# Two transformer blocks of two layers on one core: signs, a constant scale and row factors moved within the softmax steps

## What is computed

```python
# first block, top-k attention ("b") and differential attention ("c"); q and k are RMS-normalised
logits = einsum('bqhd,bqshd->bhqs', qb, k_sel) * DSA_HD ** -0.5
p = softmax(where(valid, logits, -inf))                       # "b"
logits = einsum('bqhcd,bshcd->bhcqs', qb, k) * DIFF_HD ** -0.5
p = softmax(where(allowed, logits, -inf))
attn = p[:, :, 0] - lam * p[:, :, 1]                          # "c"
# second block: scale = 1 / sqrt(64) = 1/8
q = rope(rms_norm(q, q_norm), pos)
s_c = einsum('bsghd,bngd->bsghn', q, k_cmp) * scale           # compressed keys
o_s = softmax(where(m, einsum(q, kg) * scale, NEG)) @ vg      # selected blocks
o_w = softmax(where(mw, einsum(q, kw) * scale, NEG)) @ vw     # window
o = g[..., 0:1] * o_cmp + g[..., 1:2] * o_s + g[..., 2:3] * o_w
```

## Time and profile before

| | |
|---|---|
| median of three runs | 2692.9 us (2691.5 to 2694.1) |
| the profiled execution: its own time | 2695.4 us |
| its span in the trace | 2693.6 us |
| TensorE matmuls busy | 2487.0 us, 92% |
| VectorE busy | 1395.3 us, 52%, 2981 instructions |
| ScalarE busy | 954.4 us, 35% |
| GpSimd busy | 879.1 us, 33%, 366 instructions |
| mean granted TensorE clock | 0.964 |

### The profile page before, as it was taken

How to read it: one execution, slowest core, us unless ns; L and a number is a source line. 1 busy time by engine, 2 the same in 40 slices (tenths; PEclk the granted TensorE clock), 3 DMA queues, 4 the chain that set the end, 5 groups by cost and what they waited for, 6 DMA issues and landing times.

```text
span 2693.6 us, 34184 instructions
## 1 busy us (share of the span) xinstructions
PE 2487.0 (92%) x12299; PEld 1989.3 (74%) x12303; DVE 1395.3 (52%) x2981; ACT 954.4 (35%) x1691; POOL 879.1 (33%) x366
## 2 busy tenths in 40 slices
PE   7998999899999899989988888999998888899999
PEld 6686877678868687767877557888887655788887
DVE  4587243554468734355377445454567754523335
ACT  4342243432444224343234543322224354332221
POOL 3242414234324241423422102444543200244442
PEclk9999999999999999999999889999998998999999
DMA  5232414125423241413532102444433100233332
GB/s 174 66 94 71 164 32 141 48 91 181 134 70 94 94 149 40 126 47 110 176 82 66 31 1 63 149 151 154 160 118 101 57 17 1 71 105 99 96 100 79
DMA packets 132173, 256.00 MB, mean 95 GB/s; under 512 B 21914, under 2 KB 28588, under 8 KB 132012
## 3 DMA queue, kind: packets, MB, share of 16 engines
q1 hardware_dynamic: 132012, 253.83, 29.8%
HBM read 249.60 MB, written 4.19 MB: 94 GB/s over the span
## 4 chain that ended last, share of the span: by engine, by line
PE 76%; DVE 16%; ACT 4%; issue 3%; DMA 0%; DVEq 0%; SPq 0%; ACTq 0%
PE ps L758 63%; PE ps L712 4%; PE ps L1009 1%; PE ps L905 1%; DVE arena L1705 1%; PE ps L1055 1%; DVE nsm L1418 1%; DVE top L1703 1%; PE ps L820 1%; PE ps L885 1%; DVE nsm L1416 1%; DVE ps L1644 1%; PE ps L880 1%; DVE ps L1642 1%; ACT arena L1367 1%
## 5 line engine op out<-in xcount | busy, mean ns | idle before, releaser
L688 POOL TENSOR_TENSOR wl<-raw,wh 128x1024 fp32r<-128x1024 f32 (+2 forms) x362 | 878.9, 2433 | 1788.1 <-ACT wh L1076 1787.2
L758 PE MATMUL ps<-wh,hTh 128*128 128x512 f32 (+3 forms) x1600 | 639.7, 400 | 1.2 <-DVE hTl L1648 1.2
L758 PE MATMUL ps<-wh,hTl 128*128 128x512 f32 (+3 forms) x1600 | 620.3, 388 | 0.0
L758 PE MATMUL ps<-wl,hTh 128*128 128x512 f32 (+3 forms) x1600 | 620.3, 388 | 0.0
L1076 ACT ACTIVATE wh<-raw 128x1024 fp32r<-128x1024 f32 (+2 forms) x362 | 378.4, 1049 | 522.4 <-PE ps L758 278.0
L758 PEld LDWEIGHTS ps<-wh,hTh 128*128 128x128 f32 x1600 | 307.3, 192 | 75.6 <-issue 19.7
L758 PEld LDWEIGHTS ps<-wh,hTl 128*128 128x128 f32 x1600 | 306.7, 192 | 59.5
L758 PEld LDWEIGHTS ps<-wl,hTh 128*128 128x128 f32 x1600 | 307.5, 192 | 51.3
L758 PE MATMUL ps<-hTh,wh 128*128 128x512 f32 (+2 forms) x704 | 259.0, 368 | 5.2 <-DVE hTl L1648 2.4
L758 PE MATMUL ps<-hTh,wl 128*128 128x512 f32 (+2 forms) x704 | 257.8, 366 | 0.0
L758 PE MATMUL ps<-hTl,wh 128*128 128x512 f32 (+2 forms) x704 | 257.7, 366 | 0.0
(11 more groups left out here) (271 smaller groups left out, 3251.0 us busy)
## 6 DMA issues: line engine op xcount, KB each, us to landing
raw<-in_w_in_dram SPq DMA_DIRECT2D x160, 512.0 KB, 3.6
raw<-in_w_ff_dram SPq DMA_DIRECT2D x128, 512.0 KB, 3.6
modw<-in_w_mod_dram SPq DMA_DIRECT2D x96, 512.0 KB, 4.7
raw<-in_w_br_dram SPq DMA_DIRECT2D x24, 512.0 KB, 3.7
raw<-in_w_out_dram SPq DMA_DIRECT2D x24, 512.0 KB, 3.6
xm<-in_x_dram SPq DMA_DIRECT2D x8, 512.0 KB, 4.0
raw<-in_w_out_dram SPq DMA_DIRECT2D x16, 256.0 KB, 3.8
raw<-in_w_in_dram SPq DMA_DIRECT2D x8, 408.0 KB, 3.2
```

Source lines behind the costliest of these rows:

```text
L688: pool.tensor_tensor(piece(wl, g % RING, u), piece(raw, g % RING, u), piece(wh, g % SPLIT, u).bitcast(F32), ALU.subtract)\
L758: last = pe.matmul(*args, start=(q == 0 and c == 0 and n_pass == 0), stop=(q == u["quarters"] - 1 and c == u["chunks"] - 1 and n_pass == 2))
```

## The change

Four edits, all within the softmax steps; the order of the steps, the transfers and the matmuls stay.

1. `pair_max`: the reduction writes the negated maximum directly into the bias columns, and the small multiplication by -0.125 and the wait ahead of it go. The factor 1/8 moves to the queries (edit 4).
2. `pair_prob`: the product of reciprocal and gate goes, with its wait. Each row group of the probabilities is multiplied by two column factors, the reciprocal and the gate, in one instruction: four instructions of W columns instead of one of 4W for t = 0 and 1, still two for t = 2 and 3.
3. `logit_max`: the reduction writes the negated maximum, and one product of two tensors (maxima and row factors, one column in "b", two in "c") takes the place of one or two multiplications with -1 and a factor column.
4. `q_rot` multiplies the queries by the gain and 0.125 in one instruction, and the exponentials of `pair_exp` and `cmp_logits` lose their scale of 0.125.

```diff
@@ -1347,7 +1347,7 @@
                 elif kind == "cmp_logits":
                     _, l, t = step
                     act.wait_ge(dve_result, at("cmp_shifted", l, t))
-                    act.activation(cS, cS, ACT.Exp, scale=0.125).then_inc(act_result, mark(act_result, ("cmp_exp", l, t)))
+                    act.activation(cS, cS, ACT.Exp).then_inc(act_result, mark(act_result, ("cmp_exp", l, t)))
                 elif kind == "pair_exp":
                     _, l, t, j, p = step
                     n, W, k = QUADS.index((t, j, p)), WIDTH[t], 2 * MANY[t]
@@ -1365,7 +1365,7 @@
                         for i in range(MANY[t]):
                             x, w = MANY[t] * o + i, slice(i * W, (i + 1) * W)
                             ins = act.activation(prob_of(t, n)[:, o, w], ps[:, b0 + o, w], ACT.Exp, bias=s[:, k + x:k + x + 1],
-                                                 scale=0.125, accum_out=s[:, 2 * k + x:2 * k + x + 1])
+                                                 accum_out=s[:, 2 * k + x:2 * k + x + 1])
                     ins.then_inc(act_result, mark(act_result, ("exp", l, n), ("free", logits)))
                 elif kind == "pair_turn":
                     _, l, t, j, p = step
@@ -1807,13 +1807,11 @@
                     s = soft[:, n % 8]
                     dve.wait_ge(product, at("logits", ("logits", l, m, t, h)))
                     dve.wait_ge(dve_result, at("rstd", l, m + "q"))
-                    dve.tensor_reduce(s[:, 0:k], ps[:, b0:b0 + k, 0:WIDTH[t]], AX, ALU.max)\
+                    dve.tensor_reduce(s[:, 0:k], ps[:, b0:b0 + k, 0:WIDTH[t]], AX, ALU.max, negate=True)\
                         .then_inc(dve_result, mark(dve_result))
                     dve.wait_ge(dve_result, now(dve_result))
-                    for c in range(k):
-                        ins = dve.tensor_scalar(s[:, 2 + c:3 + c], s[:, c:c + 1], -1.0, q_scale(m, t, h)[:, c:c + 1],
-                                                ALU.mult, ALU.mult)
-                    ins.then_inc(dve_result, mark(dve_result, ("bias", l, m, n)))
+                    dve.tensor_tensor(s[:, 2:2 + k], s[:, 0:k], q_scale(m, t, h), ALU.mult)\
+                        .then_inc(dve_result, mark(dve_result, ("bias", l, m, n)))
                 elif kind == "prob":
                     _, l, m, t, h = step
                     n, k, W = 4 * t + h, parts[m], WIDTH[t]
@@ -1859,7 +1857,7 @@
                     dve.tensor_tensor(x3, x3, r, ALU.mult).then_inc(dve_result, mark(dve_result))
                     dve.wait_ge(dve_result, now(dve_result))
                     if name == "eq":
-                        dve.tensor_tensor(x3, x3, hgain[:, 0].unsqueeze(1).to_broadcast([P, 8, 64]), ALU.mult)\
+                        dve.scalar_tensor_tensor(x3, x3, 0.125, hgain[:, 0].unsqueeze(1).to_broadcast([P, 8, 64]), ALU.mult, ALU.mult)\
                             .then_inc(dve_result, mark(dve_result))
                         dve.wait_ge(dve_result, now(dve_result))
                     else:
@@ -1978,14 +1976,11 @@
                     s, m = soft2[:, n % 8], MANY[t]
                     dve.wait_ge(product, at("logits", ("pair_logits", l, t, j, p)))
                     if m == 2:
-                        dve.tensor_reduce(s[:, 0:4].rearrange("p (o i) -> p o i", o=2),
-                                          ps[:, b0:b0 + 2, 0:2 * W].rearrange("p o (i w) -> p o i w", i=2), AX, ALU.max)\
-                            .then_inc(dve_result, mark(dve_result))
+                        dst = s[:, 4:8].rearrange("p (o i) -> p o i", o=2)
+                        src = ps[:, b0:b0 + 2, 0:2 * W].rearrange("p o (i w) -> p o i w", i=2)
                     else:
-                        dve.tensor_reduce(s[:, 0:2], ps[:, b0:b0 + 2, 0:W], AX, ALU.max).then_inc(dve_result, mark(dve_result))
-                    dve.wait_ge(dve_result, now(dve_result))
-                    dve.tensor_scalar(s[:, 2 * m:4 * m], s[:, 0:2 * m], -0.125, None, ALU.mult)\
-                        .then_inc(dve_result, mark(dve_result, ("bias", l, n)))
+                        dst, src = s[:, 2:4], ps[:, b0:b0 + 2, 0:W]
+                    dve.tensor_reduce(dst, src, AX, ALU.max, negate=True).then_inc(dve_result, mark(dve_result, ("bias", l, n)))
                 elif kind == "cmp_prob":
                     _, l, t = step
                     dve.wait_ge(act_result, at("cmp_exp", l, t))
@@ -2007,20 +2002,12 @@
                     dve.wait_ge(act_result, at("exp", l, n))
                     dve.reciprocal(s[:, 6 * m:8 * m], s[:, 4 * m:6 * m]).then_inc(dve_result, mark(dve_result))
                     dve.wait_ge(dve_result, now(dve_result))
-                    if m == 2:
-                        quad = lambda x: x.rearrange("p (o i) -> p o i", o=2)
-                        dve.tensor_tensor(quad(s[:, 0:4]), quad(s[:, 12:16]), part.rearrange("p (i o) -> p o i", o=2), ALU.mult)\
-                            .then_inc(dve_result, mark(dve_result))
-                        dve.wait_ge(dve_result, now(dve_result))
-                        x4 = prob_of(t, n)[:, :, 0:2 * W].rearrange("p o (i w) -> p o i w", i=2)
-                        dve.tensor_tensor(x4, x4, quad(s[:, 0:4]).unsqueeze(3).to_broadcast([P, 2, 2, W]), ALU.mult)\
-                            .then_inc(dve_result, mark(dve_result, ("prob", l, n)))
-                    else:
-                        dve.tensor_tensor(s[:, 0:2], s[:, 6:8], part, ALU.mult).then_inc(dve_result, mark(dve_result))
-                        dve.wait_ge(dve_result, now(dve_result))
-                        for o in range(2):
-                            ins = dve.tensor_scalar(prob_of(t, n)[:, o, 0:W], prob_of(t, n)[:, o, 0:W], s[:, o:o + 1], None, ALU.mult)
-                        ins.then_inc(dve_result, mark(dve_result, ("prob", l, n)))
+                    for o in range(2):
+                        for i in range(m):
+                            row, w = m * o + i, prob_of(t, n)[:, o, i * W:(i + 1) * W]
+                            ins = dve.tensor_scalar(w, w, s[:, 6 * m + row:6 * m + row + 1], part[:, 2 * i + o:2 * i + o + 1],
+                                                    ALU.mult, ALU.mult)
+                    ins.then_inc(dve_result, mark(dve_result, ("prob", l, n)))
                 elif kind == "o_split":
                     _, l, t = step
                     dve.wait_ge(act_result, at("oh", l, t))
```

## The result

| | before | changed |
|---|---|---|
| median | 2692.9 us | 2696.6 us (2695.3 to 2701.4) |
| ratio to before | | 1.0017, 95% interval 1.0010 to 1.0024 |
| profiled execution, its span | 2695.4, 2693.6 us | 2695.4, 2693.6 us |
| VectorE busy, instructions | 1395.3 us, 2981 | 1390.8 us, 2901 |
| mean granted TensorE clock | 0.964 | 0.965 |

The kernel became 3.7 us slower (the interval is 2.7 to 6.5 us). That is less than the 5.4 us named ahead as the least that counts, but it has the other sign than the 1.0 us of gain that I forecast, and 2696.6 lies beyond the 2694 where the forecast ended. So the traces are read stage by stage.

A forecast was written before the change was run, and what follows sets the result against it. TensorE, busy nearly all the time, carries 76% of the chain, VectorE 16%. Terms of -3.0 (`pair_max`, `pair_prob`), +1.9 (`logit_max`) and +0.1 (queries) gave -1.0 us: 2691.9 from 2692.9, range 2684 to 2699.

The forecast's parts named there:

- signs that I had named for being wrong: Changed profile: `logit_max` products never held, VectorE's chain pieces gone without a shorter stretch, or clock moving more than everything forecast.
- the 21 pieces of the chain: Second-block attention: places where `pair_max`'s small multiplication stands on the chain of waits; removing it gains 0.20 us each.
- I let 3.0 us through: `pair_max` and `pair_prob` together: at most 3.8 us gained, taken as 3.0 because ScalarE copies and TensorE transposes stay.
- "full gain" rival: Whole kernel: no hold, or VectorE's gain spreads; all 5.3 us come through, clock may add; 2683 to 2688, chance 0.24.
- The sum for t = 0: `pair_prob`: one multiplication of 512 becomes four of 128, 0.88 to 1.13 us; three chain pieces lose 0.25 each, 0.75.
- 0.06 us gained at t = 3: `pair_prob`, two multiplications of 512: 1.07 us before, 1.01 after, since the product of reciprocal and gate goes.
- Unit 7's bias: `logit_max` in "c", at 499.01 us: product held to the GpSimd subtraction's end, bias 0.60 us later, repeated in the other layer.
- The second place, unit 15: `logit_max` in "c", at 1219.84 us: 0.66 us of subtraction left, bias 0.34 us later, repeated in the other layer.
- Unit 11, at about 526 us: `logit_max` in "c", off the chain but short of TensorE cover: 0.4 us lost there and at its twin, 0.8 in all.
- "b" at nothing: Top-k attention's `logit_max`: eight products start inside subtractions, but the exponential waits for a transpose anyway; nothing counted.
- Part 4 at 0.1 us: Query products of 128x512 with an immediate factor: eight, four on the chain, 0 to 0.24 us lost, taken as 0.1.
- The rival "slower, by the GpSimd hold": `logit_max` holds in "c" and "b" reach the end, carried by ScalarE; up to 25 us, 2698 to 2706, chance 0.12.

The follow-up runs named there:

- Parts 1, 2 and 4: Changed kernel with `logit_max` put back as before; 2692.2 us, 0.9 under the kernel before, ratio 0.9985 to 1.0002.
- Parts 1 and 4: Kernel before with only the negated maximum in `pair_max` and the 1/8 in the queries; 2684.3 us, again 2683.1 (8.8 and 10.6 under before).
- Part 2 alone: Kernel before with only the two-factor multiplications in `pair_prob`; 2701.3 us, 7.8 over before, ratio 1.0020 to 1.0042.
- Part 3 alone: Kernel before with only the negated maximum and two-tensor product in `logit_max`; 2696.6 us, 3.5 over before, ratio 1.0004 to 1.0021.
- Part 2 at t = 2 and 3: Kernel before with negated `pair_max`, 1/8 in the queries, and two-factor `pair_prob` multiplications only at t = 2 and 3; 2688.5 us, again 2687.9.

## Why the prediction was wrong

I forecast 1.0 us gained and 3.7 us were lost. The steps, by the medians: Parts 1, 2 and 4 were to bring 2.9 us and brought 0.9; Part 3 was to cost 1.9 and cost 4.4. These two misses make up 4.5 of the 4.7 us between forecast and result. And the first hides two errors of opposite sign. One of the signs that I had named for being wrong came: the 21 pieces of the chain went and the two stages did not shorten (282.0 to 281.7 us).

- **Part 1, mechanism right, size wrong.** Each of the 21 pieces of the chain was to give 0.20 us, and the instructions do: the exponential starts 0.03 us behind the reduction and not 0.24, the reciprocal 0.08 us before its end and not 0.11 behind it. That the negated result costs nothing was right (0.69, 0.95 and 1.22 us as before). Only the sum of 4.2 us was short, and "I let 3.0 us through" went the wrong way. Parts 1 and 4 gained 8.8 and 10.6 us, 7.3 in the two stages, where TensorE's busy time for the same 706 matmuls fell from 237.0 to 232.3 us (120.01 + 117.00 against 116.99 + 115.29) and its idle time from 45.0 to 42.4. So 2.6 of the 7.3 us are less waiting, and 4.7 came with more time on the upper clock level. The "full gain" rival named this as possible and gave it 5 us at most.
- **Part 2, the step that failed.** The sum for t = 0, three pieces at 0.25 us, took the four multiplications as 1.13 us everywhere. The trace of before showed, at unit 0, the subtraction starting 0.58 us into the single multiplication of 0.69; I never laid the longer series over it, though I did just that for `logit_max`. Measured: the first transposes come 1.9 and 2.1 us later behind the first maximum than before (layers 0 and 1), with a lower clock after it. The 12 us from the maximum of unit 0 on have a granted clock of 0.57, against 0.72 in the kernel before and with Parts 1 and 4 (the changed kernel, then Parts 1 and 4):

```profile
1464.00:1476.00 12.00, 6.11 (x30) 4.89 (x31) 8.54 (x16) 5.04 (x19) 2.34 (x1) 0.57 0.00 0
```

```profile
1460.30:1472.30 12.00, 8.20 (x42) 6.63 (x43) 8.52 (x14) 5.44 (x20) 2.35 (x1) 0.72 0.00 0
```

  Part 2 alone: +7.8 us, where 0.06 us gained at t = 3 and 0.25 lost at t = 0 were the terms. The durations themselves came out as forecast (0.345 free at 128 elements, 0.41, 0.54).
- **Part 3, mechanism right, two places wrong.** 20 of the 64 products are held, none at all of the column form. Unit 7's bias was to come 0.60 us later than before and comes 1.3 later (1.64 us in place of 0.33), since I took its start within the subtraction from the earlier trace rows, where no earlier hold had pushed ScalarE. The second place, unit 15 (1219.84 us in the earlier trace rows), was to come 0.34 later and is held 0.49 us, 0.15 later, its start having moved. Unit 11, at about 526 us, was to cost 0.4 us a layer and costs 0.7. On TensorE units 6 and 7 cost 1.4 us a layer and unit 11 0.7 (Part 3 alone), 4.1 us in both, where 2.7 were in the sum.
- **"b" at nothing:** right.
- **Part 4 at 0.1 us:** the eight products of 128x512 take 693 ns with the immediate as without it, and the exponentials are as long as before. It was not tried alone.
- **The rival "slower, by the GpSimd hold"** had the right mechanism, but its 2698 was not reached. I had it act on `logit_max` alone. Of the ScalarE instructions behind the waiting exponential, which were to carry it, the rounding did, as unit 6 shows.

**Open:** why Part 2 at t = 2 and 3 costs 4 us in both comparisons. Product and multiplications together are no longer and nothing there is held; in the profiles the time goes with the clock that TensorE is granted, in different places in different executions, and not always in these stages. What sets that was not found. Nor does it add up: the costs of Part 2 on top of Parts 1 and 4, 5 to 7 us at t = 0 and 4 to 5 at t = 2 and 3, are 8 together.

## What to carry to other kernels

Before splitting one VectorE instruction into a series, or adding a second SBUF input to a small one, lay the new one over GpSimd's long instructions in the order of time: here a single one that had started got through, and a series was entered at a seam. Where a product must have two inputs, put one in PSUM if a column is free (3.0 us here by itself, nothing on top of Parts 1 and 4). Measure the parts of a change alone: here one part worth 9 to 11 us was hidden by two others.

## What was not expected of the hardware

- A GpSimd subtraction of 2.34 us started within a series of four VectorE multiplications, one every 0.26 us, and turned its 1.12 us into 3.20. The Trainium skill says, on the page and in the section named above, that `tensor_scalar` can enter a two-port mode and that whoever issues first has the shared pair for the whole instruction. The traces agree with the hold, and fit a pair that is given up between the instructions of a series: the subtraction and the fourth multiplication both start at 1467.32 us, and the fourth waits.
- Taking 0.20 us out of each of 21 pieces of the chain (4.2 us) gave 7.3 us in the stages. TensorE's idle time fell by only 2.6 of them; the rest came with more time on the upper of its two levels (1.2 and 2.4 GHz): a mean granted clock of 0.89 and 0.90 in place of 0.87 and 0.88.
- The same code took 139.8 to 145.2 us in one stage, by the clock. A single profile of a stage says nothing about 2 us.
